# A two-layer encoder step: attention of each token tile as its own stream, and the decode tile packed

## What is computed

```python
z = rms_norm(x) @ w_in                       # 1024 -> 1184 columns
q_a, k_a = rope(norm(z[:512])), rope(norm(z[512:640])); v_a = z[640:768]
cq, ckv, k_rope = norm(z[768:1024]), norm(z[1024:1152]), rope(norm(z[1152:]))
q_b = norm_rope(cq @ b_w_uq)                 # 8 heads x 96
k_nope, v_b = split(ckv @ b_w_ukv)           # 8 heads x (64 + 64), k_nope normed
o_a = softmax([q_a k_a^T / 8, sink]) v_a     # sliding window, 8 heads on 2 kv heads
o_b = softmax(q_b [k_nope, k_rope]^T) v_b    # 8 heads, chunk-causal
x += concat(o_a, o_b) @ w_o
x += swiglu(rms_norm(x))                     # layer 0; in layer 1: top 2 of 8 experts
```

## Time and profile before

| | |
|---|---|
| median of 3 runs | 1486.78 us (1485.24 to 1494.55) |
| the profiled execution | 1487.48 us, span from first to last instruction 1485.7 |
| mean granted TensorE clock | 0.922 |
| PE busy over the span | 1372.4 us (92%) |
| DVE, ACT busy | 962.5 us (65%), 802.0 us (54%) |
| attention part of layer 0 | 0 to 230 us |
| dense feed-forward of layer 0 | 230 to 447 us |
| attention part of layer 1 | 447 to 677 us |
| router and expert plan | 677 to 704 us |
| experts | 704 us to the end |

### The profile page before, as it was taken

The page is one execution under the profiler, slowest core; times in us unless marked ns, Lnnn a source line. Parts: engine busy times, 40 slices in busy tenths (PEclk is TensorE's granted clock), DMA queues, the critical chain, the costliest instruction groups (busy, mean ns, idle before and its releaser), DMA issues.

```text
span 1485.7 us, 18796 instructions
## 1 busy us (share of the span) xinstructions
PE 1372.4 (92%) x6989; PEld 1122.5 (76%) x6989; DVE 962.5 (65%) x977; ACT 802.0 (54%) x864; POOL 148.5 (10%) x130
## 2 busy tenths in 40 slices
PE   6878998999998969995999999999999999999993
PEld 3447778999994437774888888888888888888882
DVE  1555234444333464334788988889888898888984
ACT  2235333333322243332677778787777877767773
POOL 2010000000000010003001103012040120201301
PEclk9987598999998975695999999999999999999997
DMA  7032035454340040025799999999999999999995
GB/s 280 1 104 77 1 109 161 157 168 156 128 153 15 29 152 15 1 93 212 259 339 364 408 359 384 378 368 402 361 383 387 363 396 362 377 381 383 390 363 194
DMA packets 125710, 356.98 MB, mean 240 GB/s; under 512 B 8721, under 2 KB 34033, under 8 KB 125633
## 3 DMA queue, kind: packets, MB, share of 16 engines
q1 hardware_dynamic: 121120, 342.34, 62.3%
q0 software_dynamic: 4480, 14.00, 3.3%
q10 hardware_dynamic: 64, 0.02, 0.0%
HBM read 348.04 MB, written 9.48 MB: 241 GB/s over the span
## 4 chain that ended last, share of the span: by engine, by line
PE 82%; issue 6%; DVE 5%; ACT 3%; SPq 2%; DMA 1%; POOL 1%; DVEq 0%; POOLq 0%; ACTq 0%
PE ps L1638 30%; PE ps L1658 14%; PE ps L1553 10%; PE ps L1375 5%; PE ps L1528 5%; PE ps L1569 5%; PE ps L1508 3%; PE ps L1477 3%; PE ps L1489 1%; PE ps L1433 1%; PE ps L1646 1%; PE ps L1344 1%; ACT sp__65 L843 1%; SPq L577 1%; PE ps L1440 1%
## 5 line engine op out<-in xcount | busy, mean ns | idle before, releaser
L987 DVE TENSOR_TENSOR w_lo<-ring,w_hi 128x2048 fp32r<-128x2048 f32 (+1 forms) x326 | 684.6, 2126 | 187.7 <-ACT w_hi L728 184.9
L728 ACT ACTIVATE w_hi<-ring 128x2048 fp32r<-128x2048 f32 (+1 forms) x326 | 575.0, 1784 | 216.9 <-PE ps L1658 69.2
L1638 PE MATMUL ps<-w_hi,xg_hi 128*128 128x512 f32 (+1 forms) x768 | 288.9, 376 | 2.5 <-DVE xg_lo L1281 2.5
L1638 PE MATMUL ps<-w_hi,xg_lo 128*128 128x512 f32 (+1 forms) x768 | 286.8, 374 | 0.0
L1638 PE MATMUL ps<-w_lo,xg_hi 128*128 128x512 f32 (+1 forms) x768 | 286.4, 373 | 0.0
L1638 PEld LDWEIGHTS ps<-w_hi,xg_hi 128*128 128x128 f32 x768 | 145.2, 189 | 28.6 <-issue 2.9
L1638 PEld LDWEIGHTS ps<-w_lo,xg_hi 128*128 128x128 f32 x768 | 144.8, 189 | 26.0
L1638 PEld LDWEIGHTS ps<-w_hi,xg_lo 128*128 128x128 f32 x768 | 145.1, 189 | 25.3
L1658 PE MATMUL ps<-w_hi,am_hi 128*128 128x512 f32 x352 | 138.5, 393 | 0.0
L1658 PE MATMUL ps<-w_lo,am_hi 128*128 128x512 f32 x352 | 137.2, 390 | 0.0
L1658 PE MATMUL ps<-w_hi,am_lo 128*128 128x512 f32 x352 | 137.0, 389 | 0.0
(11 more groups left out here) (247 smaller groups left out, 1650.5 us busy)
## 6 DMA issues: line engine op xcount, KB each, us to landing
ring<-in_moe_w_down SPq DMA_DIRECT2D x80, 1024.0 KB, 8.2
ring<-in_moe_w_gate SPq DMA_DIRECT2D x68, 1024.0 KB, 8.9
ring<-in_moe_w_up SPq DMA_DIRECT2D x66, 1024.0 KB, 9.3
ring<-in_moe_w_gate SPq DMA_DIRECT2D x32, 768.0 KB, 7.4
ring<-in_moe_w_up SPq DMA_DIRECT2D x32, 768.0 KB, 5.9
ring<-in_ffn_w_gate SPq DMA_DIRECT2D x11, 1024.0 KB, 5.2
ring<-in_ffn_w_up SPq DMA_DIRECT2D x11, 1024.0 KB, 5.2
ring<-in_ffn_w_down SPq DMA_DIRECT2D x10, 1024.0 KB, 5.0
```

The costliest lines, as they stand in the source:

```text
L728: A(hi[:, 0:size], src[:, 0:size], ACT.Copy).then_inc(hi_ready, 1)
L987: V.tensor_tensor(lo[:, 0:size], src[:, 0:size], hi[:, 0:size].bitcast(F32), ALU.subtract).then_inc(lo_ready, 1)
L1638: ins = mm_(ps[:, b + c0 // 512, 0:c1 - c0], (xg_hi, xg_lo)[xp][:, k, :], w[wp][:, k % 2, c0:c1], start=(k == 0 and n == 0), stop=(k == KD ...
```

## The change

The order of the attention part is now three hand-written lists, one for each engine, that treat each tile as a stream of its own: the decode tile goes first, then tile 0, then tile 1. The 12 groups are 8: the decode tile and tile 0 take all eight heads in one step. A tile's projection on 512 columns is cut in two quarters (`("za", tile, half, quarter)`, 8 instructions each way), and these stand between the steps of another tile. The same holds for `wo`, which now has the tokens as stationary and 512 output columns moving, so that nothing is transposed back.

The decode tile's `za` and `wo` are packed: for each k, four matmuls of 256 columns write to four groups of 32 partitions of one bank. Its scores put four heads on 128 partitions, exponentials read PSUM, the probabilities are scaled (`dn`) before their transpose, and the values come out transposed.

ScalarE copies the projections to SBUF (`z`) beside squaring them. PSUM is three rotating pairs and two single banks, for `za` and `wo` of tiles 0 and 1. w_o takes the four slots of w_in. In layer 1 two of VectorE's splits of expert weights move behind the routing.

```diff
@@ -85,23 +85,53 @@
-ITEMS = [("k", 2), ("k", 0), ("q", 0), ("k", 1), ("q", 1), ("q", 2), ("k", 3)]
-GROUPS = [(typ, t, hg) for typ in "ab" for t in range(3) for hg in range(2)]
...
-FRONT = [("za", 0), ("tc",), ("zc", 0), ("item", 0),
...
+TILES = (2, 0, 1)
+ITEMS = [("k", 2), ("k", 3), ("q", 2), ("k", 0), ("q", 0), ("k", 1), ("q", 1)]
+GROUPS = [("a", 2, 0), ("b", 2, 0), ("a", 0, 0), ("b", 0, 0), ("a", 1, 0), ("a", 1, 1), ("b", 1, 0), ("b", 1, 1)]
...
+PE_ORDER = [("tc",), ("h", 0), ("item", 0), ("h", 2), ("za", 0, 1, 0), ("za", 2), ("za", 0, 1, 1), ("za", 0, 0, 0), ("zc", 0),
...
+ACT_ORDER = [("n1", 0), ("n1", 2), ("tce",), ("n1", 1), ("isq", 0), ("ir", 0), ("zev", 2), ("zr", 2), ("zev", 0, 1), ("zcev", 0),
...
+DVE_ORDER = [("x1", 0), ("x1", 2), ("hd", 0), ("x1", 1), ("hd", 2), ("i1", 0), ("i2", 0), ("z1", 2), ("z2", 2), ("hd", 1),
...
-        plan += [None] * (-(len(plan) + 4) % RING)
...
+        def found(key):
+
+            family, n = place[key]
+            if family == "small":
+                return small_full, small_out, n % 3, n // 3 + 1, 2 + 2 * (n % 3), 2
+            if family == "bank":
+                return bank_full, bank_out, key[3], n + 1, key[3], 1
+            return ffn_full, ffn_out, n % 4, n // 4 + 1, 2 * (n % 4), 2
...
+                kind, l, *rest = key
+                if kind == "uq":
+                    users = [("item", l, n) for n, (k_, _) in enumerate(ITEMS) if k_ == "q"]
+                elif kind == "in" and rest[0] == 2:
+                    users = [("zc", l, 0), ("zc", l, 1), ("za", l, 2)]
                 else:
...
+                    kind = "za" if kind == "in" else "wo"
+                    users = [(kind, l, 0, rest[0]), (kind, l, 1, rest[0]), (kind, l, 2)]
+                for user in users:
+                    wait_full(sp, user)
...
+                    elif kind == "zev" and which[0] == 2:
...
+                        for j in range(4):
+                            A(z[0:DEC, 2, 256 * j:256 * j + 256], pair(key)[DEC * j:DEC * j + DEC, 0:256], ACT.Copy)
+                        free(A(z[0:DEC, 2, S3:IN_W], pair(key, DEC)[:, 512:512 + IN_W - S3], ACT.Copy), key)
+                        wait_out(act, key)
+                        A(sq[0:DEC, :], z[0:DEC, 2, :], ACT.Square).then_inc(squares_z, 1)
+                    elif kind == "zev":
+
+                        t, c = which
+                        key = ("za", l, t, c)
+                        wait_full(act, key)
+                        z_free(l, t)
+                        A(sq[:, 512 * c:512 * c + 512], pair(key), ACT.Square).then_inc(squares_z, 1)
+                        free(A(z[:, t, 512 * c:512 * c + 512], pair(key), ACT.Copy), key)
...
+                    elif kind == "ir":
...
+                        act.wait_ge(mean_i, no(I_MEAN, l, ("i1", i)))
+                        w = 16 if what == "q" else 8
+                        A(sri[0:r, 0:w], sti[0:r, 0:w], ACT.Sqrt, bias=C("eps", r),
+                          scale=1.0 if what == "q" else 1.0 / NOPE).then_inc(root_i, 1)
...
+                    elif kind == "e":
...
+                        act.wait_ge(negmax_ready, no(MAXES, l, ("sm", g)))
+                        if t == 2:
+                            n, w = KVH, P + DEC
+                            src = pair(("s", l, g))
...
+                        for h in range(n):
+                            c0 = 512 * h if t == 2 else w * h
+                            ins = A(sp_[:, b, w * h:w * h + w], src[:, c0:c0 + w], ACT.Exp, bias=nb[:, g % 4, h:h + 1],
+                                    scale=scale, accum_out=rsum[:, g % 4, h:h + 1])
+                        if t == 2:
+                            free(ins, ("s", l, g))
...
+                    elif kind == "dn":
...
+                        wait_out(dve, ("s", l, g))
+                        shares(typ, g, KVH)
+                        for h in range(KVH):
+                            w = P + DEC
+                            ins = V.tensor_scalar(sp_[:, b, w * h:w * h + w], sp_[:, b, w * h:w * h + w], rden[:, g % 4, h:h + 1], None, ALU.mult)
+                        ins.then_inc(probs_ready, 1)
...
+                    elif kind == "od":
...
+                        if t == 2:
+                            wait_full(dve, key)
+                            k0 = 4 * (typ == "b")
+                            free(V.tensor_copy(hT[:, k0:k0 + 4, TOFF[2]:TOK], pair(key)[:, 0:P].rearrange("p (k c) -> p k c", k=4)), key)
+                            continue
...
+                    elif kind == "wd" and which[0] == 2:
...
+                        for j in range(4):
+                            ins = V.tensor_tensor(xres[0:DEC, 2, 256 * j:256 * j + 256], xres[0:DEC, 2, 256 * j:256 * j + 256],
+                                                  pair(key)[DEC * j:DEC * j + DEC, 0:256], ALU.add)
+                        free(ins, key)
...
+            for u in range(2, MOE_PAIRS):
+                moe_lo_part(0, u, first=True)
...
+                    elif kind == "wo" and which[0] == 2:
...
+                        for k in range(KD):
+                            for j in range(4):
+                                wk = ("wo", l, j // 2, k // 4)
+                                weights(wk)
+                                ins = mm_(pair(key)[DEC * j:DEC * j + DEC, 0:256], hT[:, k, TOFF[2]:TOK],
+                                          slot(wk, 4, 512)[:, k % 4, 256 * (j % 2):256 * (j % 2) + 256], start=(k == 0), stop=(k == KD - 1))
+                        full(ins, key)
+                    elif kind in ("za", "wo"):
+
+                        t, c, q = which
+                        key = (kind, l, t, c)
+                        if q == 0:
+                            wait_out(pe, ("h" if kind == "za" else "to", l, t))
+                            wait_room(pe, key)
+                        wk = ("in" if kind == "za" else "wo", l, c, q)
+                        weights(wk)
+                        for k in range(4 * q, 4 * q + 4):
+                            ins = mm_(pair(key), hT[:, k, TOFF[t]:TOFF[t] + P], slot(wk, 4, 512)[:, k % 4, :],
+                                      start=(k == 0), stop=(k == KD - 1))
+                        if q == 1:
+                            full(ins, key)
+                    elif kind == "zc":
...
+                            if ("ukv", l) not in seen:
+                                seen.add(("ukv", l))
                                 pe.wait_ge(ukv_ready, 16 * (l + 1))
...
+                        if t == 2:
+                            for kv in range(KVH):
+                                o = v[:, 512 * kv:512 * kv + nk]
+                                if typ == "a":
+                                    ins = mm_(o, qT2[64 * kv:64 * kv + 64, :], kTa[64 * kv:64 * kv + 64, k0:k0 + nk], start=True, stop=True)
+                                    continue
+                                for h4 in range(GRP):
+                                    h = GRP * kv + h4
+                                    ins = mm_(o[DEC * h4:DEC * h4 + DEC, :], qTb[0:QK, h, TOFF[2]:TOK], kTb[0:QK, h, k0:k0 + nk], start=True, stop=True)
+                        else:
+                            order = (0, 4, 1, 5, 2, 6, 3, 7) if t == 0 else range(4 * hg, 4 * hg + 4)
+                            for h in order:
+                                n = h - 4 * hg
+                                if typ == "a":
+                                    rows = slice(64 * (h // 4), 64 * (h // 4) + 64)
+                                    q, kk = qTa[rows, h % 4, TOFF[t]:TOFF[t] + P], kTa[rows, k0:k0 + nk]
+                                else:
...
+                        else:
+                            probs = pT[:, b, :].rearrange("p (g k h c) -> p g k h c", g=4, k=2, h=GRP)
+                            for h in range(HEADS):
+                                kv, h4 = h // GRP, h % GRP
+                                for k, kt in enumerate(kts):
+                                    ins = mm_(v[64 * (h % 2):64 * (h % 2) + 64, DEC * (h // 2):DEC * (h // 2) + DEC], value(kt, h),
+                                              probs[0:KROWS[kt], kv, k, h4, :], start=(k == 0), stop=(k == len(kts) - 1))
                         full(ins, key)
...
```

More of the change, by code:

```diff
@@ L201, in build @@
     base_fills = list(fills)
-    assert len(plan) % RING == 0
     before = {}
@@ L208, in build @@
     last_in_slot = [[k for k in plan[s_::RING] if k is not None][-1] for s_ in range(RING)]
-    used_at, tally = {}, [0] * RING
-    for n, key in enumerate(plan):
-        if key is not None and key not in DENSE:
-            tally[n % RING] += 1
-            used_at[key] = tally[n % RING]
     EXPERT = expert_plan()
@@ L359, in build @@
         warm_set = sem("warm_set")
-        loaded_x = sem("loaded_x")
+        loaded_x = [sem(f"loaded_x{t}") for t in range(3)]
+        sinks_ready = sem("sinks_ready")
         loaded_c = sem("loaded_c")
@@ L713, in _ @@
```

(34 more changed lines are left out.)

835 lines of the change are left out of this document (422 added, 413 removed), and 17 rows, old and new, of tables (ACT_ORDER, DVE_ORDER, PE_ORDER).

## The result

The changed kernel takes 1400.54 us (median of four runs, 1398.14 to 1403.56) against 1486.01 for the kernel before beside it: ratio 0.9407, 95% interval 0.9369 to 0.9444. The forecast was 1453, its range 1410 to 1492. The direction is right; the size is not: I expected 34 us less, it is 85 us less. The profiled run took 1402.91 us, with a span of 1401.1. The four runs lie in two pairs, 1398.1 and 1398.2, 1402.9 and 1403.6, and the profiled one is of the longer pair, so a difference of 5 us between two spans can be one of single runs.

What follows compares the result with a forecast made beforehand. Bound: TensorE's own work at whatever clock it gets, plus waits for a tile's square-root-and-scale chain. From 1487.5 us, layer 1 gives 31.4 less and layer 0 3.3 less: 1452.8 us; range 1410 to 1492.

Steps and rivals of the forecast that it cites:

- A: Layer 1 from the complete residual to the end of item 0: norm, cold transposes, cold item; 8.0 us.
- E: Layer 1's last add, square and root, scale, transposes and gain after the output projection: 6.1 us, before 11.6.
- B: Layer 1's projections: quarters, 160-column steps, transposes, items 1 to 3, cold start and packed decode tile; 56.8 us.
- C: Layer 1's merged middle, first scores to first output-projection quarter: 55.9 us at full clock, 87.2 with slower clock and a wait.
- D: Layer 1's output projection: 64 instructions, two values steps, two transpose blocks, cold start; 35.8 us.
- the plan: Expert plan behind layer 1's attention: two 2.28 us VectorE splits between routing and gates, about 2 covered; 3 us more.
- the packed step: Decode tile's projection and output projection, 64 instructions of 256 columns: two overlap, 0.12 us each, 7.7 us a step.
- the clock of C: Layer 1's merged middle: 39.7 us of small steps at granted clock 0.62, as in the old stage, take 64.
- the long stretch: Merged middle, item 5 through packed output projection: long matmuls at clock 1.0 once warm; 16.2 us become 19.2.
- the waits of C: Merged middle: one new wait of 4 us, for the decode tile's probabilities to be scaled before their transpose.
- rival 1: Clock stays at 2.4 GHz in the middle, about 67 instead of 87 us; 1413 us in all; chance 0.12.
- rival 3: Packed matmuls don't overlap: 1477 us; lower end, all four overlap, 17 us less: 1436; chance 0.14.

Runs made afterwards that it cites:

- experiment 1: Changed kernel with packed-step matmuls reordered: one column group after the other, 1421.50 us (0.9535); two groups alternating, 1401.83 us (0.9412).
- experiment 3: Changed kernel plus 13 unused 512-column matmuls (fillers) a layer in TensorE's waits: 1393.22 us (0.9361); 8 inside the slow stretch instead: 1409.31 us.
- experiment 5: Changed kernel with attention steps reordered: decode tile's probabilities scaled earlier, 1400.73 us; item 4's root and gains first, 1401.93 us; item 6's root earlier, 1397.09 us.

## Why the prediction missed the size

By its own steps, layer 1, forecast and measured us (A is the start up to item 0, E the last add, norm and gains): A 8.0 and 8.3 us; B 56.8 and 49.2; C 87.2 and 72.8; D 35.8 and 32.8; E 6.1 and about 5.6. Together 25 us too many, and nearly the same again in layer 0, whose middle is the same code.

- **Right:** the start of layer 0 (first quarter at 39.61 us, forecast "about 39"; item 0's end 38.62, forecast 38.6), the plan (3 us), the loop, the projections' prices, eight table loads (and one more at the start of layer 1).
- **Wrong, the packed step:** "I let two overlap and not four", 7.7 us for 64 instructions. It is 3.59 us: four overlap (experiment 1), near the 3.4 of the text's lower end. 4.1 us in each of four steps, 16 in all.
- **Wrong, the clock of C:** "the other 39.7 ... at 0.62 they take 64", and the long stretch 3 more: 27 us of clock on 55.9 us of work. C has 60.5 us of busy TensorE. With the waits filled and the clock mostly up (experiment 3, layer 0) TensorE is busy 65.0 us in C, of which 11.5 are fillers and 4.5 the low clock (a values step 5.60 instead of 3.67, transposes 1.74 instead of 0.88, item 5 3.44 instead of 1.72). That leaves, as an estimate, about 49 at full clock, so the clock cost some 11 us, where the forecast had 27. This is the largest error, 16 us a layer. The work term was 3 us too high besides the packed step: 55.9 less 4.1 is 51.8 (transposes take 0.11 us and not 0.126). The error was to carry the mean clock of the old stage to new code. The kernel before shows 1.00 from 134 to 138 us in the same kinds of step; what differs is what stands between them, and from 146 us on the steps have no gap between them in the changed order, and no values step of 32 columns.
- **Wrong, the waits of C:** 4 us forecast for one wait, 12.3 measured in five. The one foreseen (probabilities behind tile 1's rotation) is there, 5.3 us, and what ended it was not the scaled probabilities but room (experiment 5). Without the other errors this one would have made the kernel slower than forecast, by 8 us a layer. So C adds up to 49 of work, 11 of clock and 12 of waits, where the forecast had 56, 27 and 4.
- **Wrong, small:** cold starts of 2.2 us in B and in D of layer 1: the quarters start at the full-clock price there (3.63 and 3.44 us for 8).
- **The range:** rival 1 (full clock, 1413) and the lower end of rival 3 (all four overlap, 17 less) together give 1396; measured 1400.5, and the range ended at 1410. Rival 3's lower end came true. Rival 1 did not: the middle had 0.79 and not 1.00, and C took 72.8 us, where rival 1 less the packed step's 4.1 has 63. That the sum comes out so near is luck: most of those 10 us a layer are made up by cold starts and small terms of B and D that did not come. What holds is that the range was built from one rival at a time, though these two have nothing to do with each other.

What stays open is why the clock falls in one dense run of small steps and not in another: in layer 1 of the kernel with 13 fillers it fell once more at 526 us, in the last values step of tile 0, which ran at 1.00 in layer 0 of the same kernel. Of the parts of the change only the packing and the place of the quarters were undone (21 and 15 us); what the streams, the turned output projection and the copies on ScalarE are worth each is not tested.

## What to carry to other kernels

Price the clock of new code by the instructions that will stand there, long matmuls between short ones above all, and not by the mean of the stage it replaces; in this kernel the clock came back within 2 us of 512-column matmuls put into a slow stretch, and fell where real ones were taken out from between small steps. Where two terms are uncertain for unrelated reasons, let the range reach to both at their favourable ends. Before a wait is cut, find out whether it is for data or for room: undo one of the two and see whether the releaser's name stays. And read a changed step in the trace first, since cover and shifts of the clock can hide 10 us of it from the total.

## What the runs showed of the hardware

Four column groups of a 32-column fp32 stationary overlap: 3.66 us in turn, 6.28 with two in turn, 11.50 in a row for the same 64 instructions. At the low clock a values step of 32 columns costs 1.53 times (5.60 and 3.67 us), a block of 8 transposes twice (1.87 and 0.88). The granted clock of 1.00 that the profile shows from 18 to 39 us of layer 0, through 16.75 us in which TensorE does nothing, is not what the next instructions got: item 0 took 3.75 us, against 1.72 at full clock and 3.71 where the rows show 0.50. The clock fell in the midst of gapless work (106 us in the kernel with 13 fillers) and behind waits (98 us in the changed one). The Trainium skill, TensorE: Matmul & The Clock Gate, Part 4, says that the full clock doesn't engage for transposes; the trace differs, since blocks of 8 ran at half their price in tile 1's steps, among other matmuls, and the clock came back at 146 us behind 16 transposes.
